# Third expert weight issued by ScalarE at the start of each pair of blocks

## The reference

```python
MOE_EXPERTS = 64; MOE_TOPK = 2; MOE_DFF = 384

def hier_moe(h, w_group, b_group, w_expert, b_expert, w1, w3, w2):
    ...                                   # every token picks 2 of 64 experts
    def block_ffn(args):
        xb, e = args                      # a block of tokens of one expert
        return (jax.nn.silu(xb @ w1[e]) * (xb @ w3[e])) @ w2[e]
    ypad = lax.map(block_ffn, (xpad.reshape(nb, MOE_BLOCK, d), blk_e)).reshape(cap, d)
    y = jnp.zeros((n, d), h.dtype).at[tok_s].add(ypad[dest] * wgt_s[:, None].astype(h.dtype))
```

## Time and profile before

| | |
|---|---|
| median of the runs | 2673.43 us |
| profiled execution | 2670.42 us, its span 2668.6 us |
| PE busy | 2333.9 us, 87% of the span |
| mean granted TensorE clock | 0.947 of full speed |
| DMA | 724 MB, mean 271 GB/s over the span |
| expert weights | 192 transfers of 3072 KB, median 32.2 us from issue to landing |
| chain that ended last | PE 45%, DMA 38%, DVE 12% |

### The profile page before, as it was taken

How to read it: one execution, slowest core, us unless ns; L and a number is a source line. 1 busy time by engine, 2 the same in 40 slices (tenths; PEclk the granted TensorE clock), 3 DMA queues, 4 the chain that set the end, 5 groups by cost and what they waited for, 6 DMA issues and landing times.

```text
span 2668.6 us, 31794 instructions
## 1 busy us (share of the span) xinstructions
PE 2333.9 (87%) x12861; PEld 1270.5 (48%) x12861; DVE 765.4 (29%) x1158; ACT 351.7 (13%) x641; POOL 375.6 (14%) x501
## 2 busy tenths in 40 slices
PE   3999999999899999779888888888888888888882
PEld 2443344455577876544444444444444444444441
DVE  4299935423834433501101111000011011001114
ACT  2100013200422222101000000000000000000001
POOL 2266500000022200011111110011110011111100
PEclk9999999999999999789999999999999999999996
DMA  5122221121031233589999999999999999999986
GB/s 148 63 79 63 63 63 53 63 63 57 11 109 49 73 117 123 237 366 429 428 429 428 427 422 423 413 419 426 420 419 419 409 411 424 414 420 409 421 366 275
DMA packets 127328, 724.00 MB, mean 271 GB/s; under 512 B 33848, under 2 KB 93052, under 8 KB 98332
## 3 DMA queue, kind: packets, MB, share of 16 engines
q1 hardware_dynamic: 100188, 704.75, 64.4%
q0 software_dynamic: 18720, 16.84, 1.8%
q10 hardware_dynamic: 8352, 1.44, 0.4%
HBM read 724.39 MB, written 49.81 MB: 290 GB/s over the span
## 4 chain that ended last, share of the span: by engine, by line
PE 45%; DMA 38%; DVE 12%; issue 2%; ACT 1%; ACTq 1%; SPq 1%; POOL 0%; DVEq 0%; POOLq 0%
DMA big<-in_moe_w 37%; PE ps L2424 15%; PE ps L2104 13%; PE ps L2156 5%; DVE big L1138 4%; PE ps L2322 2%; PE ps L2237 1%; PE ps L2453 1%; DVE big L1268 1%; DVE big L1267 1%; PE ps L2222 1%; PE ps L1985 1%; PE ps L2343 0%; SPq L577 0%; DMA big<-h_rows,gix 0%
## 5 line engine op out<-in xcount | busy, mean ns | idle before, releaser
L2424 PE MATMUL ps<-big 128*64 128x384 f32 x4096 | 730.9, 518 | 125.0 <-DMA big<-in_moe_w 125.0
L2424 PEld LDWEIGHTS ps<-big 128*64 128x64 f32 x4096 | 356.5, 145 | 511.5 <-issue 353.7
L2104 PE MATMUL ps<-big 128*128 128x512 f32 (+2 forms) x1216 | 532.9, 597 | 3.4 <-DVE big L1133 1.7
L2453 PE MATMUL ps<-big 128*64 128x512 f32 x1536 | 365.7, 628 | 51.7 <-DVE big L1871 51.7
L2104 PEld LDWEIGHTS ps<-big 128*128 128x128 f32 (+2 forms) x1216 | 228.6, 190 | 298.4 <-issue 294.3
L1868 DVE COPY big<-ps 128x384 f32<-128x384 f32 x64 | 35.7, 557 | 810.7 <-PE ps L2424 810.7
L2453 PEld LDWEIGHTS ps<-big 128*64 128x64 f32 x1536 | 109.7, 143 | 260.1 <-issue 199.6
L2156 PE MATMUL ps<-big 128*128 128x256 f32 x768 | 187.7, 394 | 12.3 <-ACT big L890 8.4
L775 POOL COPY six<-idxs 128x1 int32 (+1 forms) x64 | 11.6, 181 | 1202.1 <-DVE big L1875 1202.1
L2156 PEld LDWEIGHTS ps<-big 128*128 128x128 f32 x768 | 143.0, 193 | 39.0 <-issue 13.4
L1875 DVE COPY big<-ps 128x512 f32<-128x512 f32 x64 | 44.2, 691 | 375.1 <-PE ps L2453 375.1
(11 more groups left out here) (387 smaller groups left out, 1692.6 us busy)
## 6 DMA issues: line engine op xcount, KB each, us to landing
big<-in_moe_w SPq DMA_DIRECT2D x192, 3072.0 KB, 32.2
big<-in_w_in SPq DMA_DIRECT2D x18, 2048.0 KB, 8.3
big<-in_w_out SPq DMA_DIRECT2D x8, 1024.0 KB, 5.9
big<-y_rows SPq DMA_DIRECT2D x8, 1024.0 KB, 10.0
big<-in_x SPq DMA_DIRECT2D x4, 1024.0 KB, 7.3
big<-in_w_out SPq DMA_DIRECT2D x8, 512.0 KB, 7.0
big<-in_x SPq DMA_DIRECT2D x16, 256.0 KB, 2.7
big<-in_w_out SPq DMA_DIRECT2D x1, 4096.0 KB, 14.7
```

Of the source, the lines that this page charges most:

```text
L2104: last = nc.tensor.matmul(ps[n % 2][0:wd, :], ring[s % 2][:, k, c:c + wd], hT[:, k, :], start=(k == 0), stop=(k == NC - 1))
L2424: last = nc.tensor.matmul(ps[2 + w][B * g:B * g + B, 0:FF], xT[k][:, j, B * g:B * g + B], W13[k][w][:, NJ * g + j, :], start=(j == 0), sto ...
L2453: last = nc.tensor.matmul(ps[5 + q][B * g:B * g + B, :], hid[k][:, m, :], W2[k][:, m, 512 * n:512 * n + 512], start=(m == 0), stop=(m == F ...
```

## The change

SyncE keeps w1 and w3 and no longer waits for `down_ok`. The w2 transfers of both blocks of a pair are issued by ScalarE, on ScalarE's own queue, at the head of its loop body for the pair, ahead of `block_(r, 0, ...)`. The waits on `down_ok` keep their numbers. Blocks 0 and 1 are loaded as before.

```diff
                 sp.wait_ge(up_ok, 2 * r + k - 1)
                 load13(bass.ds(e, 1), k)
-                sp.wait_ge(down_ok, 2 * r + k - 1)
-                load2(bass.ds(e, 1), k)
...
+            def load2(r, k):
+
+                e = act.value_load(rowi[0:1, bass.ds(2 * r + k, 1)], min_val=0, max_val=NE - 1)
+                act.wait_ge(down_ok, 2 * r + k - 1)
+                act.dma_start(W2[k], I["moe_w2"][0][bass.ds(e, 1)].rearrange("e (p c) n -> p (e c) n", c=FC)).then_inc(w2_in[k], 16)
+
...
             with act.Fori(1, NBLK // 2) as r:
                 with act.If(r < npairs):
+                    for k in range(2):
+                        load2(r, k)
                     block_(r, 0, r, 1)
                     block_(r, 1, r + 1, 0)
```

## The result

The changed kernel takes 2680.62 us (median of 8 runs, 2678.82 to 2684.05); the kernel before, timed beside it, 2672.69 (8 runs, 2669.74 to 2675.34). The ratio is 1.0031, 95% interval 1.002 to 1.0042: slower, by 8 us. Forecast were 2682 and slower.

The account below looks back on a forecast made before the run. The prediction took the DMA engines to pace the expert stage at 46.5 us a pair, TensorE close behind. 2670.4 + 4 (start) + 4 (end) + 0 = 2678.4, 2681.4 with 3.0 to the median, taken as 2682; range 2666 to 2735.

Parts of the forecast that it names:

- SyncE's freed time is worth nothing, ScalarE's issues are hidden: In each pair, SyncE's dropped issues and waits gain 0, and ScalarE's two issues and register loads cost 0.
- The path through W2[0]: From one k = 0 `down` to the next: 24.9 + 19.56 + 1.7 = 46.2 us a pair, with a new wait of about 5.3.
- Turns between two queues: While W2[0] loads, the DMA engines serve both queues by turns: landing 17.9 us, or 18.4 with gathers.
- One request that the prediction took as unmoved: In each pair, the W2 request for block 2r+1 comes when it did before the change.
- The DMA engines set the pace, middle 0: Between start and end, the DMA engines' 46.5 us a pair still rules over the new path's 46.2: loss 0.
- rival 2: No change: losses at start and end are made up by early TensorE pace and end slack; 2670 to 2678 us, chance 20%.
- The start, 4 us: Before the loop, DMA engines stand idle 4 us after about 1178.8, since no W2 is asked for there.
- The end, 4 us: In the last pair, DMA engines stand idle for the last 18 to 22 us instead of 14; 4 taken (0 to 8).
- 4 + 4 + 0 = 8: Over the whole kernel, the losses forecast: 4 us at the start, 4 at the end, 0 in between.
- Rival 1: In the loop, the path through W2[0] is longer than the DMA engines' pace; typically 2721 us, chance 28%.
- Rival 3: In the expert stage, two queues keep the DMA engines better fed: faster, 2660 or 2665 us, chance 10%.

Follow-up runs that it names:

- e6: Changed kernel, but each W2 on ScalarE asked for right after its own buffer's last `down`, and gathers issued ahead of scatters: 2679.8 us, ratio 1.0028.
- e3: Changed kernel with ScalarE's two requests swapped, W2 of block 2r+1 ahead of W2 of block 2r: 3097.9 us, ratio 1.159.
- e5: Changed kernel, but SyncE asks for w1 and w3 of the next k = 0 block only after the last one's `down`, not `up`: 2724.4 us, ratio 1.0201.
- e4: Changed kernel with 32 matmuls of unused result ahead of each k = 0 `down` from pair 1 on: 2684.1 us, ratio 1.0044.
- e2: Changed kernel with all W2 back on SyncE's queue, both of a pair still only after the `down` of block 2r-1: 2682.2 us, ratio 1.0041.
- e1: Changed kernel, but each W2, still on ScalarE's queue, asked for right after the `down` of its own buffer's last block: 2684.0 us, ratio 1.004.
- e7: Kernel before, with each gather issued ahead of the scatter that stood before it: 2672.0 us, ratio 0.9999.
- e9: Changed kernel, but W2 of block 2, the first in the loop, asked for right after the `down` of block 0: 2678.4 us, ratio 1.0022.
- e10: Changed kernel, but SyncE again asks for W2 of k = 0 on time, ScalarE only for W2 of k = 1: 2677.8 us, ratio 1.0021.

## Why the prediction came out right, point by point

- **SyncE's freed time is worth nothing, ScalarE's issues are hidden.** Right. ScalarE's two issues lie at 1796.66 to 1798.14, 7 us ahead of its next copy.
- **The path through W2[0].** Right, and nearly in every term: 0.69 from the copy's end to the request (0.4 taken), landing 18.6 (18.4), a wait of 5.8 us on average (5.3), a slow clock of 2.2 us in the pair shown (1.7), waits ahead of `up` down to nothing.
- **Turns between two queues.** Right. 18.6 lies near 17.9 for an equal share, where a 40% share would have given 22. The rule of the Trainium skill named with it (page "DMA: Bandwidth & Descriptors", section "Issuing engines are not separate DMA queues"), that moving transfers to another issuing engine saves only sequencer time, agrees as to the gain (none), and falls short as to the cost: e6, with no request a block late, is 7.1 us slower.
- **One request that the prediction took as unmoved.** W2 of k = 1 comes a little later too: second in ScalarE's pair of issues, about 2.5 us after the end of `down` (1797.8 against 1795.32 in the pair shown), where SyncE's came at once. No run shows that it costs anything.
- **The DMA engines set the pace, middle 0.** This step failed. It compared the new path, 46.2 us a pair, with one pace of the DMA engines for all 31 pairs, 46.5, and so found nothing to lose: "In between, the stock at `up`'s end falls from about 20 us of transfers to a few, but not to nothing." But 46.5 is the pace after the first pairs; the prediction's own rival 2 has 42 us a pair for those. There the path is the longer. Pairs 1 to 4 took 42.7 us each before and 47.3 after, 18.4 us in all, and pairs 5 to 30 took 46.58 and 46.59. What was taken as 0 is the whole loss. Why the time so lost is not made up later, while the DMA engines still hold requests, isn't shown; that 3.9 MB fewer were moved from 1240 to 1600 us says that they did not hold enough.
- **Which limit rules after pair 4** is open. TensorE waits for W2[0] in nearly every pair, and e3 and e5 show that more of that wait is paid in full, so the path is a limit. The DMA engines are at 98.5% of theirs. e4, which was to separate the two, doesn't. Nor do the parts add up: e2 has the lateness on one queue (98.9%, 9.9 us) and e6 the second queue (99.1%, 7.1 us), and the changed kernel has both and lost no more than e1 or e2.
- **The start, 4 us.** 408 GB/s fell to 359 from 1163 to 1194 us: 31 us x 49 GB/s = 1.5 MB, 3.6 us. The size is as forecast. But e7, which asks for its weights as the kernel before does, has 388 GB/s there, so some of it may be scatter; and that it reaches the end is only made likely by e9.
- **The end, 4 us.** Wrong in sign. The last pair is 4.5 us shorter than before. No w1 and w3 follow there, and W2[0] lands sooner: the last k = 0 `down` started at 2605.98, 13.3 us after ScalarE's request at 2592.70, having waited for it 0.4 us at most (1.24 us idle, where 0.81 is usual).
- So 4 + 4 + 0 = 8 met a measured 7.9 by a different sum. Between the two profiled spans it is -2.5 to the end of pair 0, +18.4 in pairs 1 to 4, +0.3 in pairs 5 to 30, -4.5 in the last pair and -2.1 behind it, 9.6 us. That the total was met is luck in good part: the early pairs, taken as 0, and the end, wrong in sign, cancel.
- **Rival 1** (the path is the longer) is what happened in the first four pairs, and e3 and e5 show that from there on nothing can be added to the path for free. **Rival 2** took the end's slack rightly. It trusted the early pairs to make the loss good, and they are where it arises. **Rival 3** is out: no kernel with two queues moved more in the middle than 552.5 MB, against 554.1.

## What to carry to other kernels

Where two limits lie within 1% of each other, a wait that comes or goes on the compute engine says little of the time: four kernels here wait for four different things (w1 and w3, W2, gathers, nothing) and lie within 12 us. Compare a new path with the pace of each part of a loop, not with one pace for all: here the loss fell where the kernel before still had a stock, and an average over 30 pairs hides it. An end-to-end number that comes out right doesn't prove its terms. And before a filler is used to test a wait, see that it is shorter than the wait. A second issuing engine gave no bandwidth here, and with more weights in flight the gathers landed later.

## What the runs showed of the hardware that I had not expected

- A gather's landing grows with the number of busy weight queues: 6.5 us alone, 18.3 beside one, 29.2 beside two (e1), some 11 us each. With only half of W2 on the second queue (e10) the median was 21.4.
- Weights split over two queues moved 0.6% fewer bytes in the same time than on one, no request being a block late (e6 against e7, 551.13 and 554.73 MB in 1320 us). The cause is open.
- TensorE's granted clock averaged 0.91 in the middle of the changed kernel, against 0.94 before, where it waits about 6 us at once rather than 2 to 3. With 7.4 us of filler in place of the wait (e4) it was 0.97 from 1800 to 2000 us, and the time did not fall.
